# Attention stage of a two-block transformer kernel: high weight parts by rounding transfers, gate products in three rounded parts, transposed probabilities copied by ScalarE alone

## What is computed

```python
h = rms_norm(x, norm1_g)
proj = h @ w_in      # rx, rgate, q, kc, vc, ks, vs, kw, vw, nsa_g, mg_rnn, mg_attn
hr = rg_lru(causal_dwconv(rx, rnn_conv_w, rnn_conv_b), rg_w_a, rg_b_a, rg_w_x, rg_b_x, lru_lambda)
y_rnn = (hr * jax.nn.gelu(rgate)) @ w_rnn_out
o = nsa(q, kc, vc, ks, vs, kw, vw, nsa_g, ...)
y_attn = o @ w_attn_out
x = x + (jax.nn.sigmoid(mg_rnn) * y_rnn + jax.nn.sigmoid(mg_attn) * y_attn) @ w_out
```

```python
xb = x.reshape(bsz, s, RNN_BLOCKS, RNN_BLOCK_W)
r = jax.nn.sigmoid(jnp.einsum('bsnc,ncd->bsnd', xb, w_a).reshape(bsz, s, D_RNN) + b_a)
i = jax.nn.sigmoid(jnp.einsum('bsnc,ncd->bsnd', xb, w_x).reshape(bsz, s, D_RNN) + b_x)
```

## Time and profile before

| | |
|---|---|
| median of three runs | 811.34 us |
| the profiled execution's own time | 811.55 us |
| its span in the profile | 809.8 us |
| TensorE busy | 799.9 us, 99% of the span |
| VectorE busy | 599.0 us, 74% |
| ScalarE busy | 486.6 us, 60% |
| GpSimd busy | 27.1 us, 3% |
| bytes moved by the DMA engines | 143.79 MB, mean 178 GB/s |

### The profile page before, as it was taken

How to read it: one execution, slowest core, us unless ns; L and a number is a source line. 1 busy time by engine, 2 the same in 40 slices (tenths; PEclk the granted TensorE clock), 3 DMA queues, 4 the chain that set the end, 5 groups by cost and what they waited for, 6 DMA issues and landing times.

```text
span 809.8 us, 11913 instructions
## 1 busy us (share of the span) xinstructions
PE 799.9 (99%) x4813; PEld 694.6 (86%) x4813; DVE 599.0 (74%) x773; ACT 486.6 (60%) x738; POOL 27.1 (3%) x38
## 2 busy tenths in 40 slices
PE   9999999999999999999999999999999999999996
PEld 8889998888888888988888888888888888888885
DVE  6774698998958986897878678877777665655556
ACT  6555598877767454665666566546755654544552
POOL 1102000000000000000000000020110000000000
PEclk9999999999999999999999999999999999999998
DMA  8446433342434774456555555664453655465431
GB/s 338 160 159 251 169 126 105 118 155 70 154 119 159 251 266 156 156 197 219 161 204 182 197 193 183 253 240 142 144 197 123 211 198 201 170 220 190 162 151 52
DMA packets 22630, 143.79 MB, mean 178 GB/s; under 512 B 2608, under 2 KB 3248, under 8 KB 8240
## 3 DMA queue, kind: packets, MB, share of 16 engines
q1 hardware_dynamic: 20880, 137.72, 48.0%
q10 hardware_dynamic: 1696, 5.31, 1.9%
HBM read 141.97 MB, written 1.05 MB: 177 GB/s over the span
## 4 chain that ended last, share of the span: by engine, by line
PE 92%; ACT 3%; DVE 3%; issue 1%; DMA 1%; DVEq 0%; SPq 0%; ACTq 0%
PE PS L1749 19%; PE PS L1753 10%; PE PS L1802 10%; PE PS L1803 10%; PE PS L1806 10%; PE PS L1736 5%; PE PS L1737 4%; PE PS L1741 4%; PE PS L2120 2%; PE PS L1765 2%; PE PS L2099 2%; PE PS L1859 1%; PE PS L2124 1%; PE PS L1893 1%; PE PS L1870 1%; PE PS L1773 1%
## 5 line engine op out<-in xcount | busy, mean ns | idle before, releaser
L1075 DVE TENSOR_TENSOR WL<-RAW,WH 128x2048 fp32r<-128x2048 f32 (+2 forms) x127 | 284.6, 2242 | 32.3 <-ACT WH L630 32.1
L630 ACT ACTIVATE WH<-RAW 128x2048 fp32r<-128x2048 f32 (+2 forms) x127 | 238.1, 1877 | 51.3 <-PE PS L1806 26.4
L1491 DVE TENSOR_TENSOR HLS<-PS,HLS 128x512 f32<-128x512 f32 x46 | 31.7, 689 | 92.7 <-ACT HLS L978 92.7
L1749 PE MATMUL PS<-CHL,WH 128*128 128x512 f32 x352 | 87.9, 392 | 0.0
L1736 PE MATMUL PS<-BHL,WH 128*126 128x256 f32 (+1 forms) x336 | 83.8, 287 | 0.0
L978 ACT ACTIVATE HLS<-PS 128x512 f32<-128x512 f32 x46 | 27.4, 595 | 90.8 <-PE PS L1753 86.4
L1737 PE MATMUL PS<-BHL,WH 128*126 128x256 f32 (+1 forms) x336 | 81.8, 282 | 0.0
L1749 PE MATMUL PS<-BHL,WH 128*128 128x512 f32 x320 | 79.9, 392 | 0.0
L1749 PEld LDWEIGHTS PS<-CHL,WH 128*128 128x128 f32 x352 | 63.9, 189 | 11.8
L1803 PE MATMUL PS<-WH,AHL 128*128 128x512 f32 x176 | 68.8, 391 | 0.0
L1802 PE MATMUL PS<-WH,AHL 128*128 128x512 f32 x176 | 68.7, 390 | 0.0
(11 more groups left out here) (313 smaller groups left out, 1312.3 us busy)
## 6 DMA issues: line engine op xcount, KB each, us to landing
RAW<-in_w_stream SPq DMA_DIRECT2D x108, 1024.0 KB, 4.9
RAW<-in_w_stream SPq DMA_DIRECT2D x11, 1008.0 KB, 4.8
RAW<-in_w_stream SPq DMA_DIRECT2D x8, 704.0 KB, 4.7
WF<-in_w_stream SPq DMA_DIRECT2D x2, 1024.0 KB, 5.2
LN<-in_ln ACTq DMA_DIRECT2D x2, 1024.0 KB, 5.1
...
```

What stands on the lines that cost most here:

```text
L630: eng.activation(WH[:, c % NSLOT, 0:CHUNKS[c][2]], raw(c), ACT.Copy).then_inc(w_hi, 1)
L1075: eng.tensor_tensor(WL[:, c % NSLOT, 0:CHUNKS[c][2]], raw(c), f32(WH[:, c % NSLOT, 0:CHUNKS[c][2]]), ALU.subtract).then_inc(w_lo, 1)
L1491: eng.tensor_tensor(HLS[:, n % 4, :, :], PS[:, bank:bank + 2, 0:TOK], HLS[:, n % 4, :, :], ALU.add)\
L1749: eng.matmul(PS[:, bank, :], wh, HL[:, k, :, :].rearrange("p a t -> p (a t)"), start=(k == 0), stop=False)
```

## The change

The edits concern chunks 16 to 39.

High weights: for the 23 chunks 17 to 39 (`CAST`), ScalarE no longer writes `WH`. GpSimd issues a DMA that reads the same weights a second time from HBM and rounds them on the way to `WH`. The one for chunk c + 2 is issued when chunks up to c - 1 are done, and at most two are under way. SyncE still loads `RAW`, which VectorE needs for the low part.

Low weights: VectorE makes the low part of a `CAST` chunk at the head of the iteration before it (c + 1), behind the maxima. Before, it was mostly two iterations before.

Gates: `ri` chunks are now split as well, for the first of them by ScalarE. The channels `XC` are rounded to `AH` by ScalarE (`rg_round`) and their rest goes to `AL`, by VectorE, tile by tile. Each gate product becomes three rounded ones. The small products write 106 columns, with zeros in the added ones, so these chunks grow from 588 to 716 columns (the one with three tiles from 840 to 968). TensorE waits for all low parts of a group (`rg_low`) ahead of its first gate product.

Transposed probabilities: ScalarE copies both banks in one instruction of 1024 columns, and VectorE's copy is gone.

The wait on `up2_*` semaphores becomes one on the `up_*` semaphores with an offset, with no other order of work.

```diff
-    return RG_TILES[g] * RP + HB
+    return RG_TILES[g] * RP + 64 + HB
...
-        out += [("ri", g, 2 * gate_cols(g), False)]
+        out += [("ri", g, 2 * gate_cols(g), True)]
...
+LOW_NO = [sum(1 for x in CHUNKS[:c] if x[3] and x[0] != "ri") for c in range(NCH)]
+_low_order = []
+for _c in range(NCH):
+    _low_order += [x[:2] for x in CHUNKS[_c + 1:_c + 2] if x[0] == "ri"]
+    _low_order += [x[:2] for x in CHUNKS[max(0, _c - 1):_c] if x[0] == "rnn"]
+RG_LOW_NO = {_k: _n + 1 for _n, _k in enumerate(_low_order)}
...
+CAST = [c for c in range(AT[("ri", 0)] + 1, AT[("ao", 3)] + 1) if CHUNKS[c][3]]
+HI_NO = [sum(1 for b in range(c) if CHUNKS[b][3] and b not in CAST) for c in range(NCH)]
...
-        last[slot] = SPLIT_NO[c]
+        last[slot] = c
...
+        wh_in = [sem("wh_in0"), sem("wh_in1")]
+
+        def wait_high(eng, c):
+
+            if c in CAST:
+                n = CAST.index(c)
+                eng.wait_ge(wh_in[n % 2], 16 * (n // 2) + 16)
+            else:
+                eng.wait_ge(w_hi, HI_NO[c] + 1)
+
+        def wait_both(eng, c):
+
+            wait_high(eng, c)
+            if c in CAST:
+                eng.wait_ge(raw_in[ARRIVAL[c][0]], 16 * (ARRIVAL[c][2] + 1))
...
-                        eng.wait_ge(w_lo, before + 1)
+                        if CHUNKS[before][0] == "ri":
+                            eng.wait_ge(rg_low, RG_LOW_NO[CHUNKS[before][:2]])
+                        else:
+                            eng.wait_ge(w_lo, LOW_NO[before] + 1)
...
+            for c in range(NCH):
+                if c + 2 in CAST:
+                    s, n = (c + 2) % NSLOT, CAST.index(c + 2)
+                    source = A_w[OFFS[c + 2]:OFFS[c + 3]].rearrange("(p n) -> p n", p=P)
+                    eng.wait_ge(chunk_done, c)
+                    if n >= 2:
+                        eng.wait_ge(wh_in[n % 2], 16 * (n // 2))
+                    eng.dma_start(WH[:, s, 0:CHUNKS[c + 2][2]], source).then_inc(wh_in[n % 2], 16)
...
-                if c >= NCH or not CHUNKS[c][3]:
+                if c >= NCH or not CHUNKS[c][3] or c in CAST:
...
+            def rg_round(i):
+                G, t = RG_OF[i]
+                eng.wait_ge(mb_dve, RNN_NO[i] + 1)
+                eng.activation(AH[0:RP, i, :], XC[:, G % 2, t, :], ACT.Copy).then_inc(xc_hi, 1)
...
-                eng.activation(PT[:, u % 2, 0, :, :].rearrange("p h q -> p (h q)"), PS[:, 4, :], ACT.Copy)\
-                   .then_inc(pt0_copied, 1)
+                eng.activation(PT[:, u % 2, :, :, :].rearrange("p a h q -> p (a h q)"),
+                               PS[:, 4:6, :].rearrange("p a q -> p (a q)"), ACT.Copy).then_inc(pt_copied, 1)
...
+                if c and CHUNKS[c - 1][0] == "rnn":
+                    rg_round(CHUNKS[c - 1][1])
...
-                s = SPLIT_NO[c]
-                eng.wait_ge(w_hi, s + 1)
+                wait_both(eng, c)
...
-            def unit_pt(u):
-                eng.wait_ge(t_done, u + 1)
-                if u >= 2:
-                    eng.wait_ge(pv_done, u - 1)
-                eng.tensor_copy(PT[:, u % 2, 1, :, :].rearrange("p h q -> p (h q)"), PS[:, 5, :])\
-                   .then_inc(pt1_copied, 1)
...
-                u = unit_at(w - 2)
-                if u is not None:
-                    unit_pt(u)
...
-                if c and CHUNKS[c - 1][0] == "ri" and c - 1 != SPLIT_AHEAD or c == UNIT_FIRST:
+                if c + 1 in CAST:
                     split(c + 1)
+                if c + 1 < NCH and CHUNKS[c + 1][0] == "ri":
+                    s, n = (c + 1) % NSLOT, CHUNKS[c + 1][2]
+                    wait_both(eng, c + 1)
+                    eng.tensor_tensor(WL[:, s, 0:n], raw(c + 1), f32(WH[:, s, 0:n]), ALU.subtract).then_inc(rg_low, 1)
+                if c and CHUNKS[c - 1][0] == "rnn":
+                    i = CHUNKS[c - 1][1]
+                    G, t = RG_OF[i]
+                    eng.wait_ge(xc_hi, RNN_NO[i] + 1)
+                    eng.tensor_tensor(AL[0:RP, i, :], XC[:, G % 2, t, :], f32(AH[0:RP, i, :]), ALU.subtract).then_inc(rg_low, 1)
...
-                if CHUNKS[c][:2] not in SUMS_FIRST and kind != "ri" and c != W0 and c + 1 != UNIT_FIRST or c == SPLIT_AHEAD:
+                if CHUNKS[c][:2] not in SUMS_FIRST and c + 2 not in CAST and c != W0:
...
-                    eng.wait_ge(mb_dve, RNN_THROUGH[i])
-                    w = plain(c).rearrange("p (a n) -> p a n", a=2)
+                    eng.wait_ge(rg_low, max(RG_LOW_NO["ri", i], *(RG_LOW_NO["rnn", k] for k in range(RG_AT[i], RG_AT[i + 1]))))
+                    wh, wl = (W[:, c % NSLOT, 0:2 * gate_cols(i)].rearrange("p (a n) -> p a n", a=2) for W in (WH, WL))
                     banks = {}
                     for m, t in enumerate(gate_order(i)):
+                        k = RG_AT[i] + t
                         banks[t] = mb_bank(MB_NO[c] + m)
+                        outs = [PS[0:RP, banks[t], 256 * which:256 * which + 256] for which in range(2)]
                         for which in range(2):
-                            last = eng.matmul(PS[0:RP, banks[t], 256 * which:256 * which + 256],
-                                              w[0:RP, which, RP * t:RP * t + RP], XC[:, i % 2, t, :], start=(which == 0),
+                            rows = wh[0:RP, which, RP * t:RP * t + RP]
+                            eng.matmul(outs[which], rows, AH[0:RP, k, :], start=(which == 0), stop=False, skip_group_check=True)
+                            eng.matmul(outs[which], rows, AL[0:RP, k, :], start=False, stop=False, skip_group_check=True)
+                        for which in range(2):
+                            last = eng.matmul(outs[which], wl[0:RP, which, RP * t:RP * t + RP], AH[0:RP, k, :], start=False,
                                               stop=(t == 2), skip_group_check=True)
                         if t == 2:
                             last.then_inc(ri_part, 1)
+                    first = RG_AT[i]
                     for which in range(2):
                         cols = slice(256 * which, 256 * which + 256)
-                        other = w[:, which, RP * RG_TILES[i]:gate_cols(i)]
-                        ins = eng.matmul(PS[64:64 + HB, banks[0], cols], other[0:HB], XC[0:HB, i % 2, 1, :],
-                                         start=False, stop=(which == 1), skip_group_check=True)
-                        last = eng.matmul(PS[0:HB, banks[1], cols], other[64:64 + HB], XC[64:64 + HB, i % 2, 0, :],
-                                          start=False, stop=(which == 1), skip_group_check=True)
+                        for n, (W, A) in enumerate(((wh, AH), (wh, AL), (wl, AH))):
+                            other = W[:, which, RP * RG_TILES[i]:gate_cols(i)]
+                            ins = eng.matmul(PS[0:64 + HB, banks[0], cols], other[0:HB, 0:64 + HB], A[0:HB, first + 1, :],
+                                             start=False, stop=(which == 1 and n == 2), skip_group_check=True)
+                            last = eng.matmul(PS[0:64 + HB, banks[1], cols], other[64:64 + HB, 0:64 + HB], A[64:64 + HB, first, :],
+                                              start=False, stop=(which == 1 and n == 2), skip_group_check=True)
```

85 lines of the change are left out of this document (41 added, 44 removed).

## The result

| | before | after |
|---|---|---|
| median | 811.51 us (16 runs) | 814.36 us (16 runs) |
| ratio, 95% interval | | 1.0028 (1.0020 to 1.0035) |
| profiled execution, its span | 811.55, 809.8 | 814.41, 812.7 |

The change makes the kernel slower: the medians are 2.85 us apart, and the ratio of 1.0028 is 2.3 us. On each side one disturbed execution (2043.6 and 4507.4 us) is not in the ratio. The forecast was 809.8: its range holds the result, its sign is wrong. The other times after lie in three clusters, which is why the two measures differ: three executions from 811.6 to 812.4 (mean clock 0.998), two at 812.4 and 813.1 (0.996), ten from 813.9 to 815.0 (0.993 to 0.994). The profiled one is of the last kind.

What follows compares the result with a forecast made beforehand. TensorE, busy 799.9 of 809.8 us, was taken as the bound, with VectorE second. Gates -2.9, probability copy -0.8 and a new wait +2.2 made -1.5 us, so 811.34 became 809.8, range 807.0 to 816.0.

Steps and rivals of the forecast that it cites:

- A new wait: At chunk 20, TensorE waits for VectorE's low part of chunk 18's channels: 2.2 us lost, bounds 0 and about 5.
- transfers that hold VectorE up: Rival: GpSimd's writing of transfers keeps VectorE from its operands 1 us per chunk; about +6, 815.8 us; chance 0.11.
- Gates on TensorE: Four two-tile groups gain 0.56 us each and chunk 20's three tiles 0.65: 2.9 us gained, bounds 0.1 to 3.5.
- The copy: Probabilities: with VectorE's copy gone, TensorE's one wait of 0.8 us for it goes: gain 0.8 us.
- High weights: GpSimd's rounding DMAs replace ScalarE's 19 weight copies: landing taken as 7 us, cost 0, relief of ScalarE worth 0.
- The relief is worth 0: ScalarE loses 19 high-weight copies, 36 us, but TensorE doesn't wait for them, so nothing is gained.
- The sum: Gates -2.9, copy -0.8 and new wait +2.2 give -1.5 us against the kernel before.
- pairs don't run in turn: Rival denied here: the gates' small product pairs run one after the other; gates gain 0.1, time 812.1 us; chance 0.13.
- rounding transfers aren't slow: Rival denied here: rounding DMAs land too late for chunks 16 to 36; at 18 us landing, 831 us; chance 0.06.
- No new wait: Rival: VectorE reaches chunk 20's gate parts in time through uncounted idle time; 807.6 us; chance 0.12.

Runs made afterwards that it cites:

- e8: Kernel before, with chunk 20's first gate product made to wait for VectorE's copy of the second bank of probabilities: 815.51 us, ratio 1.0044.
- e4: Changed kernel, chunk 20's gate low parts and chunk 18's channels ahead of unit 1's maxima, its exponentials behind chunk 20's first gate tile: 809.24 us, ratio 0.9972.
- e16: Kernel before, with ScalarE copying both banks of transposed probabilities and VectorE's copy gone, nothing else: 811.15 us, ratio 0.9996.
- e6: Changed kernel without rounding transfers: ScalarE writes all high weights, VectorE makes low parts in the old order; gates and copy stay changed: 818.28 us, ratio 1.0085.

## Why the prediction was wrong

**The step that failed** is "A new wait", which priced the wait at its own length, 2.2 us. Place, engine and length were about right (1.93 us at chunk 20, VectorE's low part of channels done at 124.04 against 124.1). But an idle TensorE can lose more than the time it idles: by their mean clock, 12 of 15 executions had a stretch at half clock, and a long one costs 2.7 us on top (ten around 814.5, three around 811.8). Neither sum nor rivals had a price for the clock, and that is the difference between "same as before" and the median. The second step that failed is the size of the gates' gain, forecast 2.9 and measured 1.3: it is why even the executions without a fall are not faster than before. That the range holds the median is luck: its upper end is the time of a rival, transfers that hold VectorE up, which didn't happen.

The Trainium skill ("TensorE: Matmul & The Clock Gate", what's actually happening) has the array's clock at one of two rates, the lower one being that of an engine that has been idle. The trace agrees on the levels (0.50 and 1.00), and e8's profile has the fall behind an added wait of 2.7 us alone.

**The other terms**, in the forecast's order.
- *Gates on TensorE*, forecast 2.9. Two-tile groups took 2.39 to 2.48, not 2.25: the gain was 0.42, 0.51, 0.44 and 0.33, not four times 0.56. The pairs were better than taken (0.12, not 0.14); each change of kind cost 0.1 that I hadn't counted. Chunk 20's three tiles take 3.46 without a wait (in e4: 3.68 with one of 0.22). In the changed kernel they took 5.75 (124.14 to 129.89), of which 1.3 is the half clock: from the third tile on 3.11, against 1.80 in e4. The other 4.4 hold two waits for banks, 0.7 at the third tile and 0.2 at the second, for ScalarE's copy of chunk 19 (it ends at 125.09, the second tile starts at 125.14); 0.4 was forecast. That is 4.4 against 4.01 before, a loss of 0.4. Sum 1.3, 1.6 too little.
- *The copy*, forecast 0.8: gained as said in the changed kernel, where no transpose waits. Alone it lowers the median by 0.3, which isn't clear of noise (e16), with two new waits on ScalarE; that it needs the relief of ScalarE is likely, not shown.
- *High weights*, forecast 0 for the transfers and for the relief. The transfers by themselves cost nothing that the traces show: landings of 6.4 us (7 taken), no product of TensorE held up by one, one wait of VectorE, 2.2 us at 239.5, with no wait of TensorE behind it, and low parts of 2048 columns in 2.28 us as before. The Trainium skill ("DMA: Bandwidth & Descriptors", measured bandwidth of DMAs issued from GpSimd) gives 6.15 us for 1 MB. The trace is near, with 6.4 for 1024 KB and 5.2 for 1008, rounded and beside another queue. "The relief is worth 0" was true only against the kernel before: ScalarE was 96% busy from 99 to 124 us, and the gates' rounding and the wider copy, which I added to it at no price, come late without it: e6, with the old order, is 6.8 us above before. I had read its waits, and not how full it was in that stretch.
- *A small wait* of 0.15, at chunk 17 for ScalarE's copy of the gates (line 1775), wasn't counted.
- *The sum* without a fall: -1.3 - 0.8 + 1.9 + 0.15, near 0. The three executions without one lie 0.1 to 0.8 above before; up to 0.8 is thus unexplained.

**Rivals.** GpSimd's transfers don't hold VectorE up (2.28 us a low part with and without them); pairs don't run in turn; rounding transfers aren't slow. "No new wait" is what e4 makes of the kernel. Its 809.2 against that rival's 807.6 is 0.9 of gates (2.0 gained, not 2.9), the small wait of 0.15, and 0.1 by which the kernel before was slower in these runs than in the median shown; about 0.4 stays open.
